# Hybrid encoder trunk: a new order for the opening of the attention and convolution layer

## Time and profile before

| | us |
|---|---|
| median of three runs | 1426.88 |
| profiled execution | 1427.06 |
| its span, first to last instruction | 1425.3 |
| TensorE busy / VectorE / ScalarE / GpSimd | 1363.0 / 1161.8 / 1005.7 / 64.1 |
| mean granted TensorE clock | 0.986 |

### The profile page before, as it was taken

How to read it: one execution, slowest core, us unless ns; L and a number is a source line. 1 busy time by engine, 2 the same in 40 slices (tenths; PEclk the granted TensorE clock), 3 DMA queues, 4 the chain that set the end, 5 groups by cost and what they waited for, 6 DMA issues and landing times.

```text
span 1425.3 us, 19188 instructions
## 1 busy us (share of the span) xinstructions
PE 1363.0 (96%) x6780; PEld 1146.2 (80%) x6780; DVE 1161.8 (82%) x1244; ACT 1005.7 (71%) x1166; POOL 64.1 (4%) x63
## 2 busy tenths in 40 slices
PE   5999999999879999999999999999999999989997
PEld 5866999998668888887887888888788888868876
DVE  4776655556679989998998998999899899979984
ACT  4545644445557878788788787878888787768874
POOL 1230000000040000000000000000000000000000
PEclk9999999999989999999999999999999999999999
DMA  8401954357359999989989998998999999999920
GB/s 319 178 0 32 392 209 151 119 207 266 133 180 368 353 335 395 394 323 395 395 325 392 396 396 321 397 394 321 395 393 360 357 395 394 396 336 383 363 102 30
DMA packets 175585, 427.24 MB, mean 300 GB/s; under 512 B 3760, under 2 KB 8496, under 8 KB 175408
## 3 DMA queue, kind: packets, MB, share of 16 engines
q1 hardware_dynamic: 171072, 412.10, 77.5%
q0 software_dynamic: 3024, 11.01, 2.0%
q10 hardware_dynamic: 1440, 3.48, 0.7%
HBM read 420.28 MB, written 6.29 MB: 299 GB/s over the span
## 4 chain that ended last, share of the span: by engine, by line
PE 88%; DVE 6%; ACT 3%; issue 1%; DMA 1%; ACTq 0%; SPq 0%; DVEq 0%
PE G L1209 17%; PE G L1211 17%; PE G L1210 17%; PE Y L1209 10%; PE Y L1211 10%; PE Y L1210 10%; PE G L1505 2%; DVE lo_ring L702 1%; DVE ring L764 1%; ACT hi_ring L421 1%; DMA ring<-in_w_in 1%; PE G L1303 1%; PE Y L1323 1%; DVE xT_lo L732 1%; PE G L1427 0%
## 5 line engine op out<-in xcount | busy, mean ns | idle before, releaser
L702 DVE TENSOR_TENSOR lo_ring<-ring,hi_ring 128x1024 fp32r<-128x1024 f32 x692 | 837.4, 1224 | 173.5 <-ACT hi_ring L421 131.3
L421 ACT ACTIVATE hi_ring<-ring 128x1024 fp32r<-128x1024 f32 x692 | 731.2, 1061 | 274.8 <-PE G L1211 163.4
L1209 PE MATMUL G<-hi_ring,xT_hi 128*128 128x512 f32 x896 | 356.1, 397 | 10.9 <-DVE lo_ring L702 5.8
L1211 PE MATMUL G<-lo_ring,xT_hi 128*128 128x512 f32 x896 | 350.9, 392 | 0.0
L1210 PE MATMUL G<-hi_ring,xT_lo 128*128 128x512 f32 x896 | 350.3, 391 | 0.0
L1209 PE MATMUL Y<-hi_ring,mT_hi 128*128 128x512 f32 x568 | 223.9, 394 | 0.0
L1211 PE MATMUL Y<-lo_ring,mT_hi 128*128 128x512 f32 x568 | 221.3, 390 | 0.0
L1210 PE MATMUL Y<-hi_ring,mT_lo 128*128 128x512 f32 x568 | 221.1, 389 | 0.0
L1209 PEld LDWEIGHTS G<-hi_ring,xT_hi 128*128 128x128 f32 x896 | 169.1, 189 | 47.7 <-DVE lo_ring L702 8.8
L1211 PEld LDWEIGHTS G<-lo_ring,xT_hi 128*128 128x128 f32 x896 | 169.1, 189 | 36.3
L1210 PEld LDWEIGHTS G<-hi_ring,xT_lo 128*128 128x128 f32 x896 | 169.4, 189 | 33.8
(11 more groups left out here) (227 smaller groups left out, 988.4 us busy)
## 6 DMA issues: line engine op xcount, KB each, us to landing
ring<-in_moe_wg SPq DMA_DIRECT2D x56, 2048.0 KB, 10.6
ring<-in_moe_wu SPq DMA_DIRECT2D x56, 2048.0 KB, 11.7
ring<-in_moe_wd SPq DMA_DIRECT2D x56, 2048.0 KB, 11.7
ring<-in_ffn_wg SPq DMA_DIRECT2D x5, 2048.0 KB, 7.9
ring<-in_ffn_wu SPq DMA_DIRECT2D x5, 2048.0 KB, 10.1
ring<-in_ffn_wd SPq DMA_DIRECT2D x5, 2048.0 KB, 8.3
ring<-in_ple_gate_w SPq DMA_DIRECT2D x4, 2048.0 KB, 7.9
ring<-in_w_in SPq DMA_DIRECT2D x3, 2048.0 KB, 17.4
```

The lines of the kernel that those rows point to most:

```text
L421: act.activation(hi_ring[:, n % AHEAD, :], where, ACT.Copy).then_inc(hi_done, 1)
L702: dve.tensor_tensor(lo_ring[:, n % AHEAD, :], where, hi_ring[:, n % AHEAD, :].bitcast(F32), ALU.subtract).then_inc(lo_done, 1)
L1209: pe.matmul(dst, s_hi, m_hi, start=start, stop=False, skip_group_check=True)
L1211: return pe.matmul(dst, s_hi, m_lo, start=False, stop=stop, skip_group_check=True)
```

## The change

- **Loads.** w_in comes as half 0 of a and b (256 columns of each, side by side in one chunk), q, k/v, half 1 of a and b. The first chunk is eight DMAs, two for each piece, with one semaphore for each piece; the other half chunk is two DMAs. Constants, vectors and gains have a semaphore each, and ScalarE issues the gains' DMA only after the first normalised tiles. Before those it makes hi of two pieces instead of four.
- **Projections.** Order: half 0, q, k/v, three pieces of half 1, the transposes of q and k, the last piece of half 1.
- **q and k.** Rotation and gain are folded into tables which GpSimd makes (8 products of 320 columns). q is rotated straight from PSUM and not normalised: 1/norm of q goes into the scale of the exponential, as a factor for each token and head. Squares are taken by ScalarE. k (128 columns a token tile) is normalised, then rotated. k transposed is stored with the other head's 64 partitions zero (`kT` has two versions, cleared by GpSimd), so that scores run over 128 partitions.
- **Taps.** VectorE does tiles 0 and 1, and 13 taps of tile 2 (75 in all): 14 between lo pieces, 12 after the rotation, 49 in the head loop, five a step. TensorE does the 31 of tile 3 and 18 of tile 2, all in the head loop, five a step. ScalarE makes all of TensorE's 49 diagonals, each in a buffer of its own. VectorE adds TensorE's part of tile 2 to its own at the end.
- **Lo pieces** 14 to 17 (of w_out) move from the projections into the head loop.

The added lines, cut to their core (`taps(todo, n)` issues the next n taps of a list; the lines that they replace are in the functions printed above):

```diff
+    out = [("w_in", "ab", 0, 4), ("w_in", "q", 0, 4), ("w_in", "kv", 0, 2), ("w_in", "ab", 1, 4),
...
+SHARED = 13
+PE_TAPS = tuple((3, k) for k in range(CONV_W)) + tuple((2, k) for k in range(SHARED, CONV_W))
+EARLY_TAPS = tuple((c, k) for k in range(13) for c in range(2))
+LATE_TAPS = tuple((c, k) for k in range(13, CONV_W) for c in range(2))
+LATE_TAPS = tuple(x for n, t in enumerate(LATE_TAPS) for x in ((t,) if n % 2 or n // 2 >= SHARED else (t, (2, n // 2))))
+EARLY_DIAGS = 9
...
+        def load_ab(n, first, last, done):
+            dst = ring[:, slot_of(n), :].rearrange("p (k h n) -> p k h n", k=KT, h=2)
+            for half in range(2):
+                at = 768 + half * CONV_CH + DENSE[n][2] * 256
+                sp.dma_start(dst[:, first:last, half, :], w_in[:, first:last, at:at + 256]).then_inc(done, 16)
+        for s in range(4):
+            load_ab(0, 2 * s, 2 * s + 2, first_in[s])
         for n, chunk in enumerate(DENSE):
+            if n == 0:
+                continue
...
+            if chunk[1] == "ab":
+                load_ab(n, 0, KT, slot_in[slot_of(n)])
...
+                filled, value = (slot_in[s], 16 * fills_of(c)) if c else (first_in[n], 32)
+                hi(n, filled, value, ring[:, s, off:off + PIECE])
...
+        hi_upto(1)
+        act.wait_ge(vec_in, 16)
         norm_hi(0, Y8)
+        act.dma_start(qk_gain, a["qk_gain"].broadcast_to([P, QK])).then_inc(qk_gain_in, 16)
...
+        hi_upto(2 + AHEAD)
+        act.activation(unused[:, 0:1], eps[:, 0:1], ACT.Sigmoid)
+        act.wait_ge(pe_piece, 4)
+        act.activation(sig_b, G8[:, 4:6, :], ACT.Sigmoid).then_inc(sig_done, 1)
+        for n in range(3, 7):
+            hi_upto(n + AHEAD)
+            diagonals(3 * (n - 3))
         act.wait_ge(pe_piece, 8)
+        act.activation(sq[:, :, 0:512], Y[:, 0:2, :], ACT.Square).then_inc(q_sq, 1)
+        act.activation(unused[:, 0:1], eps[:, 0:1], ACT.Sqrt)
+        hi_upto(8 + AHEAD)
+        act.wait_ge(pe_piece, 10)
+        act.activation(sq[:, :, 512:QK], Y[:, 2:4, 0:P], ACT.Square).then_inc(k_sq, 1)
+        act.activation(v_sb[:, :, :], Y[:, 2:4, P:2 * P], ACT.Copy).then_inc(qkv_copied, 1)
+        hi_upto(9 + AHEAD)
         act.wait_ge(qk_ss, 1)
...
+        act.activation(unused[:, 1:2], eps[:, 0:1], ACT.Sigmoid)
+        hi_upto(11 + AHEAD)
+        act.wait_ge(qk_rot, 1)
+        diagonals(EARLY_DIAGS + 6)
         act.wait_ge(qk_tr, 1)
         act.activation(qT[:, :, :], Y[:, 0:2, :].rearrange("p b (k n) -> p (b k) n", k=2), ACT.Copy).then_inc(qk_tr_copied, 1)
+        act.wait_ge(k_zero, 1)
+        for u in range(2):
+            half = slice(u * HEAD_DIM, (u + 1) * HEAD_DIM)
+            act.activation(kT[half, :, u, :], Y[half, 2, :].rearrange("p (k n) -> p k n", k=2), ACT.Copy).then_inc(qk_tr_copied, 1)
+        act.wait_ge(pe_piece, 14)
+        act.wait_ge(glu_done, 1)
+        act.activation(sig_b, G8[:, 6:8, :], ACT.Sigmoid).then_inc(sig_done, 1)
+        act.activation(unused[:, 0:1], eps[:, 0:1], ACT.Exp)
+        hi_upto(13 + AHEAD)
...
+                                   scale=qk_scale[:, t * 10 + i:t * 10 + i + 1],
...
+            diagonals(EARLY_DIAGS + 6 + 4 * (i + 1))
...
+        glu(0)
+        lo_upto(3 + AHEAD)
+        for n in range(4, 7):
+            taps(early, 4)
             lo_upto(n + AHEAD)
+        taps(early, 2)
+        def rope_of(src, heads, first):
+            for m, c in ((0, 0), (1, 1), (2, 1), (3, 0)):
+                ins = dve.tensor_tensor(rope[:, m, :, first:first + heads, :], src[:, :, :, c, :],
+                                        table[:, :, first:first + heads, m, :], ALU.mult)
+            link(ins)
+        def rotated(dst, heads, first, c):
+            m, op = ((0, ALU.subtract), (2, ALU.add))[c]
+            return dve.tensor_tensor(dst, rope[:, m, :, first:first + heads, :], rope[:, m + 1, :, first:first + heads, :], op)
+        dve.wait_ge(q_sq, 1)
+        dve.wait_ge(table_set, 8)
+        rope_of(Y[:, 0:2, :].rearrange("p t (n c f) -> p t n c f", c=2, f=HALF), HEADS, 0)
...
+        for c in range(2):
+            rotated(q_out[:, :, :, c, :], HEADS, 0, c)
+        ss_t = s_small[:, 0:20].rearrange("p (t n) -> p t n", t=T)
+        for t in range(T):
+            dve.tensor_reduce(ss_t[:, t, 0:HEADS], sq[:, t, 0:512].rearrange("p (n f) -> p n f", f=HEAD_DIM), AX.X, ALU.add)
+        lo_upto(7 + AHEAD)
+        dve.wait_ge(k_sq, 1)
+        for t in range(T):
+            ins = dve.tensor_reduce(ss_t[:, t, HEADS:], sq[:, t, 512:QK].rearrange("p (n f) -> p n f", f=HEAD_DIM), AX.X, ALU.add)
+        ins.then_inc(qk_ss, 1)
+        lo_upto(8 + AHEAD)
         dve.wait_ge(qk_std, 1)
...
+        for t in range(T):
+            ins = dve.tensor_tensor(k_n[:, t, :].rearrange("p (n f) -> p n f", f=HEAD_DIM),
+                                    Y[:, 2 + t, 0:P].rearrange("p (n f) -> p n f", f=HEAD_DIM),
+                                    ss_t[:, t, HEADS:].unsqueeze(2).broadcast_to([P, KV_HEADS, HEAD_DIM]), ALU.mult)
         link(ins)
+        dve.tensor_scalar(qk_scale[:, 0:20], s_small[:, 0:20], HEAD_DIM ** -0.5, None, ALU.mult)
+        dve.tensor_scalar(qk_scale[:, 20:40], s_small[:, 0:20], -HEAD_DIM ** -0.5, None, ALU.mult)
+        rope_of(k_n.rearrange("p t (n c f) -> p t n c f", c=2, f=HALF), KV_HEADS, HEADS)
+        k_out = rot[:, :, 512:768].rearrange("p t (n u c f) -> p t n u c f", u=2, c=2, f=HALF)
+        for c in range(2):
+            for u in range(2):
+                ins = rotated(k_out[:, :, :, u, c, :], KV_HEADS, HEADS, c)
         ins.then_inc(qk_rot, 1)
+        lo_upto(9 + AHEAD)
+        taps(early, len(early))
+        glu(1)
+        nqk = qk_scale[:, 20:40].rearrange("p (t n) -> p n t", t=T)
         for i in range(HEADS + 2):
...
+                dve.tensor_tensor(s_small[:, 44 + 2 * b:46 + 2 * b], s_small[:, 40 + 2 * b:42 + 2 * b], nqk[:, i, :],
+                                  ALU.mult).then_inc(neg_done, 1)
+            if i >= 2 and i % 2 == 0:
+                lo_upto(9 + i // 2 + AHEAD)
+            taps(late, 5)
...
+        taps(late, len(late))
+        dve.wait_ge(conv_mm, 2)
+        dve.wait_ge(conv_v[2], SHARED)
+        dve.tensor_tensor(conv[:, 2, :], conv[:, 2, :], G[:, 2, 0:SEQ], ALU.add).then_inc(conv_v[2], 1)
...
+        pool.memset(kT[:, :, :, :], 0.0).then_inc(k_zero, 1)
+        pool.wait_ge(cst_in, 16)
+        pool.wait_ge(qk_gain_in, 16)
+        gain = qk_gain.rearrange("p (n c f) -> p n c f", c=2, f=HALF)
+        for t in range(T):
+            for m, (angle, c) in enumerate(((cos, 0), (sin, 1), (cos, 1), (sin, 0))):
+                pool.tensor_tensor(table[:, t, :, m, :], gain[:, :, c, :],
+                                   angle[:, t, :].unsqueeze(1).broadcast_to([P, QK // HEAD_DIM, HALF]), ALU.mult).then_inc(table_set, 1)
...
+        def ab_channels(n0, half, pieces):
+            for s in pieces:
+                pe.wait_ge(lo_done, n0 + s + 1)
+                w_hi, w_lo = piece_at(hi_ring, n0 + s, 512), piece_at(lo_ring, n0 + s, 512)
+                for r in range(2):
+                    k = 2 * s + r
+                    if half == 0:
+                        pe.wait_ge(nlo_done, k + 1)
+                    for f in range(4):
+                        ins = three(G8[:, 2 * half + (f // 2) * 4 + f % 2, :], w_hi[:, r, f * P:(f + 1) * P],
+                                    w_lo[:, r, f * P:(f + 1) * P], xT_hi[:, k, :], xT_lo[:, k, :],
+                                    k == 0 and f % 2 == 0, k == KT - 1)
+                piece(n0 + s, ins)
...
+        ab_channels(0, 0, range(4))
+        cols_tokens(4, 4, lambda t: Y[:, t, :], 512)
+        cols_tokens(8, 2, lambda t: Y[:, 2 + t, 0:256], 256)
+        ab_channels(10, 1, range(3))
         pe.wait_ge(qk_rot, 1)
+        pe.wait_ge(qkv_copied, 1)
...
         ins.then_inc(qk_tr, 1)
+        ab_channels(10, 1, range(3, 4))
...
+        def conv_taps(first, last):
+            for n in range(first, min(last, len(PE_TAPS))):
+                c, k = PE_TAPS[n]
+                pe.wait_ge(diag_a, n + 1)
+                alone = n + 1 == len(PE_TAPS) or PE_TAPS[n + 1][0] != c
+                ins = pe.matmul(G[:, c, 0:SEQ], diag_of(n), upad[:, c, k:k + SEQ],
+                                start=n == 0 or PE_TAPS[n - 1][0] != c, stop=alone)
+                if alone:
+                    ins.then_inc(conv_mm, 1)
+        pe.wait_ge(qk_tr_copied, 3)
+        pe.wait_ge(glu_done, 2)
         for i in range(HEADS + 2):
...
                 for t in range(T):
+                    ins = pe.matmul(Y[:, i % 2, t * SEQ:(t + 1) * SEQ], qT[:, i // 2, t * P:(t + 1) * P],
+                                    kT[:, i // 4, i % 2, :], start=True, stop=True)
                 ins.then_inc(sc_done, 1)
+            conv_taps(5 * i, 5 * i + 5)
...
```

(61 more changed lines are left out.)

150 lines of the change are left out of this document (42 added, 108 removed).

## The result

The changed kernel took 1407.03 us, the median of four runs (1406.51 to 1407.96), against 1426.93 for the kernel before in the same session (1424.85 to 1428.25): a difference of 19.90 and a ratio of 0.9868, with a 95% interval of 0.985 to 0.9885. The forecast was 1409.0 with a range of 1405.8 to 1415.0.

The account below looks back on a forecast made before the run. Bound before the mean: the first chunk's load, then VectorE, then TensorE in the head loop. Start 6.7, projections 20.2, loop -8.3, tail -0.1, GpSimd -0.4 give 18.1: 1427.06 to 1409.0, own range 1406.5 to 1411, with rivals 1405.8 to 1415.0.

Parts of the forecast that it names:

- The start: Opening: first projection matmul at 12.7 instead of 19.39, as pieces of the first chunk land apart; gain 6.7 us.
- rival 1: First load: its pieces land together or 1 KB runs are slow, first matmul at 18.5, total 1414.8; chance 0.12.
- the bound of 18.5: Opening: latest start of the first projection matmul, if the eight DMAs share the queues and land together.
- Projections: First projection matmul to first scores: 45.0 instead of 65.2 us, VectorE leaving the path; gain 20.2.
- Head loop: First scores to last output: 43.2 instead of 34.9 us, with 49 taps on TensorE, which stays the bound; loss 8.3.
- the half clock of the first piece: First projection piece: 5.21 us, nearly all at the 1.2 GHz level, kept as before.
- Tail and rest: Loop end to the mean: 1.35 instead of 1.28, a loss of 0.1; mean to end unchanged at 1304.6 us.
- rival 5: Behind the mean: FFN weights or a wait take back 5 us or so, total 1414; chance 0.04.
- GpSimd: Folded tables: eight products of 0.75 us, ready at 28 to 34; 0.4 us charged for holding up VectorE.
- 2: Projections or head loop: VectorE becomes the bound, total 1413.6 or 1413.0; chance 0.20.
- 3: First projection piece: TensorE's clock rises sooner, piece takes 2.9 us, total 1406.7; chance 0.12.
- 4: Head loop: clock stays at half after TensorE's idle before the first scores, loop doubles, total 1452; chance 0.02.

Follow-up runs that it names:

- e1: The changed kernel, but ScalarE waits for all four pieces of the first chunk before its first hi copy: 1412.18 us.
- e6: The changed kernel, but the scores run over 64 partitions as before, without the padding: 1408.08 us.
- e8: The changed kernel with v padded by zeros to 128 columns, so that output matmuls use the whole array: 1404.52 us.
- e9: The changed kernel itself, run again on the chip of the last experiments: median 1406.61 us, ratio 0.9863 to the kernel before.
- e7: The changed kernel, but GpSimd builds its eight table products twice and VectorE waits for both sets: 1408.92 us.
- e4: The changed kernel with six more tap-like instructions on VectorE ahead of lo 11: 1408.39 us.
- e3: The changed kernel, but all four pieces of half 1 are projected before the transposes of q and k: 1408.98 us.
- e5: The changed kernel, but TensorE's taps go to tiles 3 and 2 in turn for 36 of the 49: 1406.70 us.
- e10: The changed kernel with six matmuls on zeros before the first transposes: median 1409.61 us, ratio 0.9889 to the kernel before.
- e12: The changed kernel with v padded, two lo pieces before the loop, a later gate-product wait and six early matmuls on zeros: 1406.26 us, ratio 0.9863.

## Why the prediction was right, point by point

**The start**, 12.7 forecast, 13.16 measured. Pieces land apart (rival 1 is out): piece 1 was there at 10.3, not 9.9, and the hi copy, lo piece and tile behind it took 2.85 where the steps gave 2.8. The queues' rate from 9 to 12 us was 350 GB/s, as the forecast had taken it. e1 shows that without the separate semaphores it would be 17.0; the bound of 18.5 for that case was 1.5 too high.

**Projections**, 45.0 to first scores, measured 45.3. The order of events is as forecast: half one ends at 27.5 (26.6), q at 38.4 (37.5), k,v at 44.1 (43.3), the third piece at 52.8 (51.9). The offset is the start's 0.46 and a half one of 14.30 instead of 13.87, whose half-clock stretch lasted a little longer, and nothing else. lo 11 ended at 45.6 against a need at 47.0: 1.4 to spare, as worked out for an opening at half clock; e6 and e8 show 0.6 for a fast one. Rotation was done at 49.8, 2.9 before its need, the forecast's figure too. These lines of VectorE's timeline, lo 11 and the rotation's last instructions, bear it:

```profile
44.39 1.21 DVE L739 TENSOR_TENSOR lo_ring<-ring,hi_ring 128x1024 fp32r<-128x1024 f32 x1
...
48.96 0.90 DVE L825 TENSOR_TENSOR ring<-ring 128x128 f32<-128x128 f32 x4
```

**Head loop**, the step that was mis-sized: 43.2 forecast, 41.26 measured. The term is the tap: 49 x 0.48 = 23.6 against 49 x 0.432 + 2 x 0.2 = 21.6. The 0.48 came from dividing a group of the earlier trace rows by its count, when 0.20 of it was the split's and paid once. The scores' 1.0 was right as a mean and wrong as a price: 1.10 once, 0.86 twice and 1.06 five times. Without this miss the forecast would have read 1407.0 for a profiled execution that took 1407.96. VectorE was busy for 36.9 of the 41.3, against a forecast of 37.5 of 43.2.

**Luck.** The loop gave back 1.9 less than forecast, and against that the start gained 0.5 less, the projections 0.3 less, and 0.4 was lost behind the mean. So the total is closer than its largest term. And the forecast kept the half clock of the first piece (5.21), which this profile happened to have in full; four of the eleven profiles without warm-up don't, and there the opening is 2.6 shorter. The lowest of all executions of this kernel, 1404.85 in e9, lies below the forecast's range. The mechanism was right: what it named as leaving the path left it, and TensorE was the bound where it said so.

**Tail and rest.** 1.45 against 1.35; the distance from the mean to the end is 1305.0 against 1304.6, so the gain arrives whole (rival 5 is out), and the medians, 19.9 apart, say the same. A single profile could hardly show it: this distance was 1302.5 to 1306.6 in the profiles without warm-up.

**GpSimd**, charged at 0.4: the products took 1.21 each on average (0.87 with VectorE idle) instead of 0.75 and started at 18.7 instead of 22, since the gains landed earlier. They were done at 28.3, inside the 28 to 34 given. The two errors cancel. Beside them lo pieces took 1.59 and 1.88 instead of 1.23, in time that VectorE had free, so the 0.4 cost nothing on this path. The exclusive lock that the Trainium skill's page "SBUF - State Buffer" describes under "Who interferes with whom" would make each engine wait for the other, and in e7 both do: products of 0.87 take 1.23, taps of 0.41 take 1.04. The full length of an instruction is not what VectorE waited, though: 0.6 is less than a product alone, and the measurement decides.

**Rivals.** 2 did not occur in the changed kernel, but e4, with 3.1 us more on VectorE, e7 and e8 each reach it, so 0.20 was no overstatement. 3 occurs in some executions of this opening (e4, e6, e7, e8) and not in others; it is worth 2.6, the 2.3 I gave it and a little more. 4 did not: TensorE idled 1.5 before the first scores and the clock stayed at 1.00; in e6 it fell for some 4 us after the same wait, and rose again under the loop's work. The chances as I gave them add up to 1.01.

## What to carry to other kernels

A group's time divided by its count is a price only if nothing is paid once per group: compare groups of two sizes or with different neighbours first. When TensorE can't be kept busy, put a piece of matmul work that needs nothing new between a producer and the copies that read it: here that was worth 2.15 us for moving one call. And count a wait of TensorE at up to twice its length: half clock behind it cost as much again in e4 and half as much in e7, but nothing in e3. Compare edits by interval, because a single total carries such episodes from elsewhere; and before a slow stretch is blamed on an edit, look for it in a profile of the kernel without the edit.

## What the runs showed of the hardware

- The first fp32 matmul behind a change between 64 rows or columns and the full array took 0.20 us more (taps 2.36 against 2.16, scores 1.06 against 0.86).
- The length of a wait doesn't tell what the clock does behind it. One of 2.6 us was followed by 6 us at half clock (e4) and one of 3.5 by 3.4 (e7), but one of 3.6 by none (e3). One of 1.5 us was followed by none (the changed kernel, e1, e5) or by about 4 us (e6).
- At the start of a span the granted clock reads 1.00 while matmuls stand 0.21 apart.
- The load of the q/k gains, in among the first chunk's, took the queues from 384 to 169 GB/s for a microsecond and made the first piece 1.6 us late.
- GpSimd's product of 128 x 320 took 0.87 us alone and 1.2 beside two-input VectorE instructions; a VectorE tap beside it took 1.04 instead of 0.41.
- Six early matmuls made the twelve transposes behind them 1.3 us shorter and the whole kernel 3 us longer (medians), with a wait of 1.8 to 1.9 us (at 1244.8 in e10, 1241.9 in e12) that no other profile has and for which none shows a releaser.
